# Gate and up projections of the feed-forward layers computed feature-major from the second chunk on

## What is computed

```python
D_MODEL, SEQ, D_FF = 1024, 256, 2816

def rms_norm(x, w):
    y = x * lax.rsqrt(jnp.mean(x * x, axis=-1, keepdims=True) + EPS)
    return y * w

def swiglu(h, w_gate, w_up, w_down):
    return (jax.nn.silu(h @ w_gate) * (h @ w_up)) @ w_down

x = x + 0.5 * swiglu(rms_norm(x, norm_w[i, 0]), ffn_w_gate[i, 0], ffn_w_up[i, 0], ffn_w_down[i, 0])
```

## Time and profile before

| | us |
|---|---|
| median of 3 runs (lowest to highest) | 1296.69 (1296.36 to 1298.89) |
| the profiled execution | 1296.14 |
| its span in the trace | 1294.0 |
| TensorE products busy, 6910 of them | 1270.7 (98%) |
| VectorE busy | 756.8 (58%) |
| ScalarE busy | 673.5 (52%) |
| granted TensorE clock | 0.999 of full speed |
| read from HBM | 222.06 MB, 172 GB/s over the span |

### The profile page before, as it was taken

The page is one execution under the profiler, slowest core; times in us unless marked ns, Lnnn a source line. Parts: engine busy times, 40 slices in busy tenths (PEclk is TensorE's granted clock), DMA queues, the critical chain, the costliest instruction groups (busy, mean ns, idle before and its releaser), DMA issues.

```text
span 1294.0 us, 18221 instructions
## 1 busy us (share of the span) xinstructions
PE 1270.7 (98%) x6910; PEld 1088.7 (84%) x6910; DVE 756.8 (58%) x883; ACT 673.5 (52%) x901; POOL 126.8 (10%) x198
## 2 busy tenths in 40 slices
PE   9999999999999999999999999989999999999997
PEld 7888889999788888888888888877888888999896
DVE  5655645876895645554555544765655554666654
ACT  6545435658884544443544534853654443444554
POOL 3000000027730000000000001620000000000000
PEclk9999999999999999999999999999999999999999
DMA  9656645464446456554565463422566565564421
GB/s 301 209 180 211 217 145 196 138 222 131 163 166 224 138 188 195 195 203 154 195 194 177 177 219 108 161 66 81 180 195 208 188 205 163 154 193 176 149 112 49
DMA packets 181852, 224.03 MB, mean 173 GB/s; under 512 B 8857, under 2 KB 133118, under 8 KB 181790
## 3 DMA queue, kind: packets, MB, share of 16 engines
q1 hardware_dynamic: 179614, 218.01, 51.0%
q10 hardware_dynamic: 1888, 5.01, 1.2%
q0 software_dynamic: 288, 0.15, 0.0%
HBM read 222.06 MB, written 1.08 MB: 172 GB/s over the span
## 4 chain that ended last, share of the span: by engine, by line
PE 88%; DVE 5%; ACT 3%; issue 1%; DMA 1%; SPq 1%; POOL 0%; ACTq 0%; DVEq 0%; POOLq 0%
PE acc L625 27%; PE acc L627 27%; PE acc L626 27%; PE tr L642 4%; DVE w_lo L1981 1%; ACT w_hi L1372 1%; DMA raw<-in_ffn_w_up 1%; DVE conv L2251 1%; PE aux L1080 1%; PE tr L939 1%; PE acc L1061 1%; ACT xT_hi L1384 0%; ACT E L1577 0%; ACT junk L1438 0%; SPq L487 0%
## 5 line engine op out<-in xcount | busy, mean ns | idle before, releaser
L1981 DVE TENSOR_TENSOR w_lo<-raw,w_hi 128x2048 fp32r<-128x2048 f32 (+2 forms) x187 | 420.4, 2274 | 182.2 <-ACT w_hi L1372 182.1
L1372 ACT ACTIVATE w_hi<-raw 128x2048 fp32r<-128x2048 f32 (+2 forms) x189 | 351.7, 1895 | 118.5 <-PE acc L627 117.4
L625 PE MATMUL acc<-w_hi,xT_hi 128*128 128x512 f32 (+1 forms) x914 | 362.4, 396 | 0.7 <-DVE w_lo L2600 0.4
L627 PE MATMUL acc<-w_hi,xT_lo 128*128 128x512 f32 (+1 forms) x914 | 355.1, 389 | 0.0
L626 PE MATMUL acc<-w_lo,xT_hi 128*128 128x512 f32 (+1 forms) x914 | 354.4, 388 | 0.0
L625 PEld LDWEIGHTS acc<-w_hi,xT_hi 128*128 128x128 f32 x914 | 171.9, 188 | 36.3 <-issue 1.8
L627 PEld LDWEIGHTS acc<-w_hi,xT_lo 128*128 128x128 f32 x914 | 171.6, 188 | 36.1
L626 PEld LDWEIGHTS acc<-w_lo,xT_hi 128*128 128x128 f32 x914 | 172.1, 188 | 32.9
L625 PE MATMUL acc<-w_hi,hT_hi 128*128 128x512 f32 x448 | 176.1, 393 | 0.3 <-DVE y_sb L2500 0.3
L627 PE MATMUL acc<-w_hi,hT_lo 128*128 128x512 f32 x448 | 174.6, 390 | 0.0
L626 PE MATMUL acc<-w_lo,hT_hi 128*128 128x512 f32 x448 | 174.5, 389 | 0.0
(11 more groups left out here) (300 smaller groups left out, 1129.6 us busy)
## 6 DMA issues: line engine op xcount, KB each, us to landing
raw<-in_ffn_w_down SPq DMA_DIRECT2D x88, 512.0 KB, 4.7
raw<-in_ffn_w_gate SPq DMA_DIRECT2D x86, 512.0 KB, 4.0
raw<-in_ffn_w_up SPq DMA_DIRECT2D x86, 512.0 KB, 5.2
raw<-in_ssm_w_in SPq DMA_DIRECT2D x48, 512.0 KB, 4.5
raw<-in_w_in_a SPq DMA_DIRECT2D x64, 256.0 KB, 4.0
raw<-in_ssm_w_out SPq DMA_DIRECT2D x16, 512.0 KB, 4.3
E<-decay_rows ACTq DMA_DIRECT2D x8, 512.0 KB, 5.3
raw<-in_mla_w_out SPq DMA_DIRECT2D x8, 512.0 KB, 4.3
```

The costliest lines, as they stand in the source:

```text
L625: pe.matmul(o, lh, rh, start=start, stop=False, skip_group_check=skip)
L627: return pe.matmul(o, ll, rh, start=False, stop=stop, skip_group_check=skip)
L1372: inst = act.activation(w_hi[:, u % RING, 0:n], raw[:, u % RING, 0:n], ACT.Copy)
L1981: inst = dve.tensor_tensor(w_lo[:, u % RING, 0:n], raw[:, u % RING, 0:n], w_hi[:, u % RING, 0:n].bitcast(F32), ALU.subtract)
```

## The change

Chunk 0 of each layer is still computed token-major, but into the two `aux` banks. From chunk 1 on the roles are swapped: the weight tile (128 inputs by 128 columns) is loaded into the array and x is streamed. With `w_hi` loaded, one product of 512 columns streams x's high and low half one behind the other, which are now one tensor `xT`, into one bank, left half and right half; with `w_lo` loaded, a product of 256 columns streams the high half alone, onto the left half. A chunk has four feature tiles (two of gate, two of up) and eight k tiles, so 32 products of 512 and 32 of 256 columns. Odd chunks take the four `acc` banks, even ones the two `tr` and two `aux` banks.

The result stands feature-major, so no turn follows. ScalarE copies the right halves out (`gb`, `ub`), VectorE adds the left halves to them (`gs` for gate, `h` for up), multiplies gate with `rB`, ScalarE makes silu, VectorE the product, ScalarE `hT_hi`, VectorE `hT_lo`. `rB` is `rstd` as a row on all partitions, made once a layer by two TensorE products. Up is no longer scaled by `rstd`; the sums at the end are scaled by `half_rstd`, half of `rstd`, instead of by 0.5. In the first layer `turn_rows` comes behind the first piece of the down projection and waits for the last reads of `aux`. The last of the diff's places keep counts of pairs and turns (one pair fewer and one turn more a layer).

```diff
-        xT_hi, xT_lo = overlaid(("xT_hi", [P, KD, T], F32R), ("xT_lo", [P, KD, T], F32R))
+        (xT,) = overlaid(("xT", [P, 2, KD, T], F32R))
+        xT_hi, xT_lo = xT[:, 0], xT[:, 1]
...
+        half_rstd = sb("half_rstd", [P, 4, TB])
...
+        _, gs, rB, gb, ub = overlaid(("_f1", [P, 4 * D], F32), ("gs", [P, 2, T], F32), ("rB", [P, T], F32),
+                                ("gb", [P, 2, T], F32), ("ub", [P, 2, T], F32))
...
+                        o = aux[:, tb, :] if spare else bank(p, tb)
+                        last = product(o[:, 0:width], source[0][:, k0 + kk, ts], source[1][:, k0 + kk, ts],
                                        w_hi[:, u % RING, w], w_lo[:, u % RING, w],
                                        k0 + kk == 0, k0 + kk == kt - 1)
...
-                with pe.Fori(0, NC // 2) as i:
-                    for j in range(2):
-                        u, p = u0 + 2 + 2 * j, p0 + 1 + j
-                        for b in range(TB):
-                            claim(p, b, i)
-                        token_unit(u, p, 0, 4, KD, 512, lap=4 * i)
-                        h_turn(k0 + j, i)
-                        token_unit(u + 1, p, 4, 4, KD, 512, lap=4 * i)
...
-                sum_units((hT_hi, hT_lo), KF, lambda n: turn_done(pe, k0 + n),
-                          middle=lambda: h_turn(k0 + NC - 1))
+                def chunk_half(u, k_first, gate_bank, up_bank, lap, marks=False):
+                    pe.wait_ge(lo_ready, u + 1 + lap)
+                    for kk in range(4):
+                        k = k_first + kk
+                        for g, bank_of in enumerate((gate_bank, up_bank)):
+                            for ft in range(2):
+                                w = slice(kk * 512 + g * CW + ft * P, kk * 512 + g * CW + ft * P + P)
+                                o = bank_of(ft)
+                                pe.matmul(heads(o, 2), w_hi[:, u % RING, w], xT[:, :, k, :], start=k == 0, stop=False,
+                                          skip_group_check=True)
+                                last = pe.matmul(o[:, 0:T], w_lo[:, u % RING, w], xT[:, 0, k, :], start=False,
+                                                 stop=k == KD - 1, skip_group_check=True)
+                                if marks and g == 0 and kk == 3:
+                                    last.then_inc(turned, 1)
+                    last.then_inc(unit_used, 1)
+
+                def acc_half(half, lap):
+                    chunk_half(u0 + 2 + half, 4 * half, lambda ft: bank(p0, ft), lambda ft: bank(p0 + 1, ft), 4 * lap)
+
+                def claim_acc(lap):
+                    for p in (p0, p0 + 1):
+                        for b in range(2):
+                            claim(p, b, lap)
+
+                def spare_chunk(lap):
+                    for b in range(2):
+                        claim_turn(k0 + 2 + (b - k0) % 2, lap)
+                        pe.wait_ge(aux_read[b], a0 + 1 + lap)
+                    for half in range(2):
+                        chunk_half(u0 + 4 + half, 4 * half, lambda ft: tr[:, ft, :], lambda ft: aux[:, ft, :], 4 * lap,
+                                   marks=half == 1)
...
+                claim_acc(0)
+                acc_half(0, 0)
+                for tb in range(TB):
+                    pe.wait_ge(aux_read[tb], a0 + 1)
+                turn([(ft * T + tb * P, h[:, tb, ft * P:(ft + 1) * P]) for ft in range(2) for tb in range(TB)], k0)
+                claim_turn(k0 + 1)
+                for tb in range(TB):
+                    last = pe.matmul(tr[:, (k0 + 1) % 2, tb * P:(tb + 1) * P], rstd[:, tb:tb + 1].to_broadcast([P, P]),
+                                     ident[:], start=True, stop=True)
+                last.then_inc(turned, 1)
+                acc_half(1, 0)
+                spare_chunk(0)
+                with pe.Fori(1, NC // 2) as i:
+                    claim_acc(i)
+                    acc_half(0, i)
+                    acc_half(1, i)
+                    spare_chunk(i)
...
+                def last_rows():
+                    if f == 0:
+                        pe.wait_ge(rows_landed, 16 * (len(row_parts) - 1))
+                        for b in range(2):
+                            pe.wait_ge(aux_read[b], a0 + 6)
+                        for tile in row_tiles[1:]:
+                            turn_rows(*tile)
+
+                def hidden_ready(n):
+                    if n:
+                        pe.wait_ge(hidden_done, 10 * f + n)
+                    else:
+                        turn_done(pe, k0)
+
+                sum_units((hT_hi, hT_lo), KF, hidden_ready, middle=last_rows)
...
+                act.wait_ge(unit_used, u0 + 2)
+                for tb in range(TB):
+                    act.activation(sg[:, tb, :], aux[:, tb, 0:CW], ACT.Silu, scale=rstd[:, tb:tb + 1]).then_inc(gated, 1)
+                split_to(u0 + 6)
+                act.wait_ge(turned, k0 + 1)
+                act.activation(hT_hi[:, 0:2, :].rearrange("p f t -> p (f t)"), tr[:, k0 % 2, :], ACT.Copy)\
+                    .then_inc(turn_hi, 1)
+                act.wait_ge(turned, k0 + 2)
+                turn_free(act.activation(rB[:], tr[:, (k0 + 1) % 2, 0:T], ACT.Copy), k0 + 1)
                 with act.Fori(0, NC // 2) as i:
                     for j in range(2):
-                        gate(j, i)
-                        for v in range(2):
-                            split(u0 + 4 + 2 * j + v, 4 * i)
-                        hidden_high(j, i * 4 + 2 * j, i)
-                c.split = u0 + 2 * NC + 2
-                gate(NC - 1)
-                split_to(u0 + 2 * NC + 4)
-                hidden_high(NC - 1, 2 * (NC - 1))
-                c.unit, c.pair, c.turn = u0 + 2 * NC, p0 + NC, k0 + NC
+                        act.wait_ge(unit_used, i * 4 + (u0 + 2 * j + 4))
+                        act.activation(gb[:], (tr if j else acc[:, 2 * (p0 % 2):2 * (p0 % 2) + 2, :])[:, :, T:2 * T], ACT.Copy)                            .then_inc(gate_copied, 1)
+                        act.activation(ub[:], (aux if j else acc[:, 2 - 2 * (p0 % 2):4 - 2 * (p0 % 2), :])[:, :, T:2 * T], ACT.Copy)                            .then_inc(up_copied, 1)
+                        split(u0 + 6 + 2 * j, 4 * i)
+                        act.wait_ge(gate_scaled, i * 2 + (10 * f + j + 1))
+                        act.activation(sg[:], gs[:], ACT.Silu).then_inc(gated, 1)
+                        split(u0 + 7 + 2 * j, 4 * i)
+                        act.wait_ge(hidden_made, i * 2 + (10 * f + j + 1))
+                        act.activation(hT_hi[:, bass.ds(i * 4 + (2 + 2 * j), 2), :], h[:], ACT.Copy).then_inc(turn_hi, 1)
...
-                    acc_free(dve.scalar_tensor_tensor(xs, bank(c.pair + tb, nh), scale, xs, ALU.mult, ALU.add),
+                    by = scale if isinstance(scale, float) else scale[:, tb:tb + 1]
+                    acc_free(dve.scalar_tensor_tensor(xs, bank(c.pair + tb, nh), by, xs, ALU.mult, ALU.add),
...
+                halved = note(dve.tensor_scalar(half_rstd[:, f, :], rstd[:], 0.5, None, ALU.mult))
+                for tb in range(TB):
+                    dve.wait_ge(gated, g0 + tb + 1)
+                    dve.tensor_tensor(h[:, tb, :], aux[:, tb, CW:2 * CW], sg[:, tb, :], ALU.mult)\
+                        .then_inc(aux_read[tb], 1)
+                split_to(u0 + 6)
+                dve.wait_ge(turn_hi, h0 + 1)
+                turn_free(dve.tensor_tensor(hT_lo[:, 0:2, :].rearrange("p f t -> p (f t)"), tr[:, k0 % 2, :],
+                                            hT_hi[:, 0:2, :].rearrange("p f t -> p (f t)").bitcast(F32),
+                                            ALU.subtract), k0)
+                turn_done(dve, k0)
+                turn_done(dve, k0 + 1)
+                a0 = 6 * f
+
...
                 with dve.Fori(0, NC // 2) as i:
                     for j in range(2):
-                        hidden(j, i)
-                        for v in range(2):
-                            split(u0 + 4 + 2 * j + v, 4 * i)
-                        hidden_low(j, i * 4 + 2 * j, i)
-                c.split = u0 + 2 * NC + 2
-                hidden(NC - 1)
-                split_to(u0 + 2 * NC + 4)
-                hidden_low(NC - 1, 2 * (NC - 1))
-                c.unit, c.pair, c.turn = u0 + 2 * NC, p0 + NC, k0 + NC
-                c.high, c.gate = h0 + NC, g0 + 2 * NC
+                        dve.wait_ge(gate_copied, i * 2 + (10 * f + j + 1))
+                        for ft in range(2):
+                            inst = add_halves(gs[:, ft, :], tr[:, ft, :] if j else bank(p0, ft), gb[:, ft, :])
+                            if j:
+                                inst.then_inc(tr_read[ft], 1)
+                            else:
+                                acc_free(inst, p0, ft)
+                        dve.wait_ge(up_copied, i * 2 + (10 * f + j + 1))
+                        for ft in range(2):
```

(29 more changed lines are left out.)

64 lines of the change are left out of this document (23 added, 41 removed).

## The result

| | before | after |
|---|---|---|
| median (lowest to highest, runs) | 1296.92 (1296.20 to 1299.49, 19) | 1302.73 (1298.96 to 1305.69, 19) |
| ratio of after to before | | 1.0037 [1.0029, 1.0045] |
| the profiled execution | 1296.14 | 1301.53 |
| its span | 1294.0 | 1299.8 |

A forecast was written before the change was run, and what follows sets the result against it. TensorE's stream of products was taken as the bound: -19.0 us for turns, +8.5 for more products, +0.9 for `rB`, and 0.2 of waits gave -9.4 us, so 1287.3 us was predicted, range 1284.3 to 1292.

The forecast's parts named there:

- The turns that go: On TensorE, 40 of 44 turns (transposes of `h`) go at 0.474 us each, 19.0 us less.
- 512 columns cost 0.2268 wherever they stand: On TensorE, a 512-column product takes 0.2268 us: its columns and 13.4 ns an instruction, whatever its width.
- the new scale: In the sums at the end, a column replaces a constant in the same instruction, at a cost of 0.
- rival (a): The two-piece stream of x costs as two products: 16.9 us more in all, 1304.2 us, slower; chance 4%.
- The pair at 0.3468: In the swapped chunks, a 512-wide and a 256-wide product together take 0.2268 + 0.1200 us; 8.5 us more over 40 chunks.
- Rival (d): Smaller gain: alternating widths add 1 to 3 ns a product, 1290 to 1295 us; 12% for a smaller gain, 5% for none.
- `rB` at 0.22 us a layer: Two fp32 products a layer on TensorE make `rB`, at 0.11 us each; 0.9 us in all.
- The cover: VectorE's and ScalarE's new work hides behind TensorE: VectorE's 9.1 us sequence fits the 11.10 us period; cost nothing.
- (b): Weight loads become TensorE's limit: 1.1 us a chunk more than forecast, 1330 us, slower; chance 1%.
- (c): VectorE's sequence outgrows the chunk's period, at 11.5 us costing 16 us, 1303 us; chance 2%.
- (e): More gain, 1284 us: `rB` hidden, waits nil, and other 512-wide products 1 ns faster; chance 5%.

The follow-up runs named there:

- e10_scale_last: The changed kernel with `half_rstd` allocated behind everything, so that all old tensors have their old places; 1295.04 us, 0.9983 of before.
- e3_one_piece: The changed kernel with `hT` 64 bytes behind its old place and x's halves side by side, streamed in one piece; 1300.78 us, 1.0031 of before.
- e12_one_piece_last: `e10_scale_last` with x's halves side by side, so a wide product streams one piece; 1295.07 us, 0.9985 of before.
- e9_narrow128: The changed kernel with `hT` at +128 bytes and each 512-wide product of the feature-major chunks made as two of 256 columns; 1311.31 us, one run.
- e2_before_shift: The kernel before with 32 unused bytes a partition behind `rstd` and nothing else changed; 1304.51 us, 1.0058 of before.

## Why the prediction was wrong

**The turns that go: right.** 16 transposes of `h` are left of 176. The down projection of `e10_scale_last` is 0.47 us shorter than before (60.76 for 61.21 to 61.25 in layers 2 and 3), which is the price of one turn, 0.474, in a stage where nothing else changed.

**512 columns cost 0.2268 wherever they stand: wrong.** This and the pairs together turned the sign; without it the result is 0.9983. The prediction costed the stages without a diff at nothing and the new scale at "a column for a constant in the same instruction: 0". The instruction costs nothing; its 32 bytes cost 8.9 us by count, 8.2 by the stages and 7.7 by the medians of after and `e10_scale_last`, because they stand ahead of `hT_hi` in the allocation. No rival held this; that 1302.73 us lies near the 1304.2 of rival (a) is chance. The argument "13.4 ns are the same at both widths, so they belong to the instruction, not to the address" was drawn from rows in which all distances between tiles were alike, so no row could tell.

**The pair at 0.3468: right in one layer, mis-sized in three.** It measured 0.3467 in one layer of the changed kernel and 0.3533 in three: 960 x 6.5 ns = 6.2 us. The prediction's last words named this as what would make it wrong, pairs that aren't at the sum of both distances. Rival (d), alternating widths, is what happened, but not as a few ns on each product: it is 0 or 6.6 ns a pair, layer by layer.

**`rB` at 0.22 us a layer: mis-sized, it takes twice that.** TensorE of the changed kernel in layer 2:

```profile
441.43 0.28 PE L849 MATMUL acc<-xT,w_lo 128*128 128x256 f32 x1
441.55 0.60 PE L652 MATMUL tr<-ident,h 128*128 128x128 f32 x4
441.98 0.61 PE L878 MATMUL tr<-ident,rstd 128*128 128x128 f32 x4
442.35 0.48 PE L847 MATMUL acc<-xT,w_hi 128*128 128x512 f32 x1
442.67 0.28 PE L849 MATMUL acc<-xT,w_lo 128*128 128x256 f32 x1
```

The two products of L878 leave four records, so a plain fp32 product leaves two. The earlier trace rows said so already: its x4 of L930 are four records of two products (the loop of L930 makes one per token block), which the prediction read as four products; and the 0.43 us ahead of that group are those of the four transposes. So 0.11 us was the price of a record, not of a product. The break takes 442.67 - 441.43 - 0.12 - 0.227 = 0.89 us where a turn alone took 0.45: `rB` costs 0.44 a layer, nearly the upper end that was given (0.45), 0.9 us more in all.

**The cover: right.** One chunk on VectorE and on ScalarE in the changed kernel; `gb` at 57.03 is t = 0:

```profile
57.66 0.75 DVE L2190 TENSOR_TENSOR gs<-acc,gb 128x256 f32<-128x256 f32 x2 [3.32 <-ACT gb L1551]
58.33 0.75 DVE L2190 TENSOR_TENSOR h<-acc,ub 128x256 f32<-128x256 f32 x2
58.99 0.68 DVE L2213 TENSOR_TENSOR gs<-gs,rB 128x512 f32<-128x512 f32 x1
59.95 2.29 DVE L2036 TENSOR_TENSOR w_lo<-raw,w_hi 128x2048 fp32r<-128x2048 f32 x1 [0.28 <-ACT w_hi L1429]
62.16 0.68 DVE L2222 TENSOR_TENSOR h<-h,sg 128x512 f32<-128x512 f32 x1
62.76 2.28 DVE L2036 TENSOR_TENSOR w_lo<-raw,w_hi 128x2048 fp32r<-128x2048 f32 x1
64.97 0.68 DVE L2226 TENSOR_TENSOR hT_lo<-h,hT_hi 128x512 f32 x1
```

```profile
57.03 0.60 ACT L1551 ACTIVATE gb<-acc 128x512 f32<-128x512 f32 x1 [4.72 <-PE acc L849]
...
59.81 0.63 ACT L1555 ACTIVATE sg<-gs 128x512 f32<-128x512 f32 x1
60.32 1.92 ACT L1429 ACTIVATE w_hi<-raw 128x2048 fp32r<-128x2048 f32 x1
62.99 0.63 ACT L1558 ACTIVATE hT_hi<-h 128x512 f32 x1 [0.75 <-DVE h L2222]
```

The first split is ready at t = 5.2 (5.4 forecast), the second at 8.0 (8.4), the sequence ends at 8.6 (9.1), and it fits the period with 2.7 us to spare. VectorE is busy 7.72 us (8.3), ScalarE 5.84 (6.0). TensorE waits for `w_lo` as before.

**The rivals.** (a) fell with `e3_one_piece` and `e12_one_piece_last`: one piece and two cost the same. (b) fell too. In a stretch of `e9_narrow128` with nothing but 256-wide products the weight loads (second pair) are busy for all of it, and the products keep 0.1200:

```profile
60.00:70.00 10.00, 10.00 (x85) 10.00 (x85) 6.19 (x6) 4.32 (x6) 0.00 (x0) 1.00 0.56 185
```

(c) fell with the timeline above. (e), `rB` hidden and a better pace, didn't come.

**The sum.** The down and out-projections grew by 6.7 us in the table, and 8.6 with the four turns they lost; 0.4 of it is in the first layer's, which is as long in `e10_scale_last` (61.32) although nothing is displaced there, so the displacement has 8.2. -9.4 forecast, +8.6 for them, +6.2 for the pairs, +0.9 for `rB` make +6.3, and the spans differ by 5.8. Small terms of both signs are left. Gate/up of the first layer is 1.5 us shorter than the terms make it, as it took 1.8 us more than in the next layers before and 0.5 after; the start is 0.4 us later, and some other stages are up to 0.2 us shorter each. And the attention and gate/up of layer 4 are about 1 us longer: a stretch there ran in part with the clock at half speed (`PEclk`, third number from the end) in the profile of after:

```profile
850.00:855.00 5.00, 4.64 (x28) 3.35 (x27) 3.29 (x6) 2.95 (x5) 3.15 (x2) 0.66 0.65 210
```

(1 - 0.66) x 2 x 5.00 = 3.4 us at 1.2 GHz for 2.4, so at most 1.7 us lost. Every profile of an experiment has at least one such stretch too and that of before has none inside the work, but the runs' mean clocks are alike (0.995 to 0.999 for before, 0.996 to 0.999 for after), and why it falls where it does was not tried.

The question that the prediction didn't ask is which tensors a new allocation moves. The diff showed it: one line between `rstd` and `hT_hi`.

## What to carry to other kernels

A new tensor is a change to every tensor allocated behind it: put it last, or compare the starts of the loaded and the streamed tile modulo 256 bytes before and after, and look at a stage that the change doesn't touch first. The sum of single costs is safe for products only as long as their order is one that the trace shows; where widths are mixed, try the equal ones behind each other: here it took the difference between layers away and cost little against the best of them. And when a part that must be the same isn't, test the old kernel with nothing but the side effect: `e2_before_shift` took one line and settled most of the case.

## What the hardware showed

The distance between the loaded and the streamed tile matters: 226.7 ns for a 512-wide product at 0 and 256 bytes, 233.3 at 32 and 64, 232.4 at 128. The Trainium skill (TensorE: Matmul & The Clock Gate, Step-by-step: what each phase is for) says that TensorE reads SBUF through two independent ports, one for the streamed operand and one for weight loads, so that loading the next tile takes no SBUF read bandwidth from the running product. By that alone the distance between the two tiles wouldn't matter, and in these runs it costs up to 6.6 ns a product, 2.9%; whether the reads meet in the memory or the delay arises elsewhere they don't show. Products of 256 columns took 120.0 ns behind one another; all that were looked at have their tiles at distance 0 modulo 256.

The mean distances lie on steps in most streams: 120.0, 226.7, 233.3, 346.7 and 353.3 ns are 18, 34, 35, 52 and 53 times 6.67 ns. It is no rule for each product: 232.4 ns at 128 bytes isn't such a multiple, the grouped streams lie between, and in a layer at 353.3 single pairs take 0.35 and 0.36 us.

A plain fp32 product of 128x128 leaves two records, 0.11 us each, and so costs 0.22.
